# Block two's recurrence input and gate tiles: joint passes over the high part of the weights

## The chip, the cores and the metric

One Trainium2 chip, of which the kernel uses one core. The metric is the device time of one execution in microseconds. Below, PE (TensorE) multiplies matrices, PEld is its weight load, ACT is ScalarE, DVE is VectorE, POOL is GpSimd, and SP issues the DMA loads.

## What is computed

Two blocks, each run for two layers, on 256 tokens of width 1024. The change touches only the mixer of block two, of which this matters (f32 throughout):

```python
def rms_norm_2(x, g):
    xf = x.astype(jnp.float32)
    y = xf * lax.rsqrt(jnp.mean(xf * xf, axis=-1, keepdims=True) + EPS)
    return (y * g.astype(jnp.float32)).astype(x.dtype)
...
        h = rms_norm_2(x, mix_norm[i])
        proj = h @ w_in[i]
        rx, rgate, q, k, v, f_logit, ga, gb = jnp.split(proj, split_idx, axis=-1)

        rx = causal_dwconv(rx, conv_w[i], conv_b[i])
        ya = rg_lru(rx, rg_wa[i], rg_ba[i], rg_wx[i], rg_bx[i], rg_lambda[i])
        ya = (ya * jax.nn.gelu(rgate)) @ w_rnn_out[i]
        yb = forgetting_attention(q, k, v, f_logit, f_b[i], q_norm[i], k_norm[i]) @ w_attn_out[i]
```

`rx` is the input of the recurrence and `rgate` its gate: 1024 columns each of the product with `w_in`. `rg_lru` begins with two block-diagonal products of `rx` and a sigmoid on each. The feed-forward layers stand before and behind the mixer, and the first block has a mixer of its own; neither is touched.

## The kernel before

**Weights.** All weights come in tiles of 128 x 2048 numbers (1 MB). A tile goes through a fixed line: SP loads it into one of four `raw` buffers (L448) once the tile four places earlier has been used; ACT copies it to `hi`, rounded to the type fp32r (`pump`, L1125); DVE subtracts to get the rest, `lo`, into the place of `raw` (`pump`, L1671); then PE may use it. The activations are held the same way, x = x_hi + x_lo. A product is hi·x_hi + hi·x_lo + lo·x_hi. `pump(n)` on ACT or DVE makes all tiles up to number n, at that place of the engine's instruction stream; every engine works strictly through its own stream, and waits on semaphores.

**Form B.** A tile that gives 256 output features by 256 tokens is multiplied in one of two ways. `form_b` (L556) keeps both halves of 128 features in one PSUM bank; for each half and each of eight slices of the contraction it runs three matmuls of 256 columns (L578 to L580), 48 in all. `joint_b` (L583) gives each half of the features its own bank, two banks in all. x_hi and x_lo lie side by side, so one matmul of 512 columns (L592) multiplies the high weights with both, eight for each half; then eight of 256 columns (L595) add lo·x_hi on the left half of the bank, 32 in all. The left half then holds hi·x_hi + lo·x_hi and the right half hi·x_lo, and someone must add them: ACT copies the right halves out (`low_half`), DVE adds them to the left ones (`both_halves`). `joint_b` is used before in the feed-forward layers and for most tiles of the output mixer.

**The stretch.** In block two, each layer runs: feed-forward in and out, `va` (2 tiles), `rx` (4 tiles, recurrence input), `rg` (4 tiles, gate), `fl` (a narrow one, 8 columns), then eight block-diagonal pairs of matmuls (L1048, the products of `rg_lru`), then `q`, `k`, `vb`. In this text rx0 to rx3 and rg0 to rg3 are the tiles of the two jobs, q0 to q3 those of `q`.

- PE: rx0 to rx3 in banks 0 to 3, rg0 to rg3 in banks 0 to 3 again, `fl` in bank 0, all by `form_b`. L1048 for feature group f goes to bank 4 + f % 4, once the convolution of f is there and, from f = 4 on, once ACT has read the bank (`rg_ev`). q0 and q1 write banks 2 and 3.
- DVE: for tile j, first `used(tile)`: `pump` two tiles ahead, then wait for PE. Then a multiply with the row of 1/rms (`times_root`, L1721). For `rx` the convolution follows (L2200, L2203: eight instructions on 256 columns), for `rg` nothing. After `fl` the forget gate's arithmetic (from L2215).
- ACT: for `rx` only its `pump`; then two small functions for the decay (L1556, L1557); for each `rg` tile `pump` two ahead, wait for DVE's multiply, gelu in place (L1562). Then `pump` to q1, and 16 sigmoids on the L1048 products (L1568), of which the first needs its function table loaded.
- After the sigmoids DVE makes `la` and `ii` (L2221, L2222), ACT takes the tanh of `la` (L1572) and only then pumps q2, which DVE turns to `lo` and PE multiplies.

The order on each engine is the order of the code, written by hand. `take(b)` makes PE wait for what last released bank b.

Of the kernel before, what the change touches and what calls it, by code (L numbers as in the profile page):

```python
# [14 lines left out]
P = 128  # L15
# [45 lines left out]
    "gl_ready": (4, 4), "mg_in": (8, 8), "xf_ready": (0, 0), "sum_in": (33, 53), "half_ev": (33, 53),  # L61
# [129 lines left out]
def build_program(nc, dram):  # L191
# [3 lines left out]
    with ctx:  # L195
# [231 lines left out]
        def halves(b, n):  # L427

            return banks[b // 2][:].rearrange("p (f n s) -> p f n s", f=2, n=2)[:, :, n, :]

# [112 lines left out]
        def _(pe):  # L543
# [477 lines left out]
            for layer in range(DEPTH):  # L1021
# [13 lines left out]
                for name in ("rx", "rg"):  # L1035
                    for b, tile in enumerate(BY2[name]):
                        form_b(tile, x_in, b)
                        freed[b] = scaled.next()
                form_b(BY2["fl"][0], x_in, 0)
                freed[0] = scaled.next()  # L1040
# [75 lines left out]
        def _(act):  # L1116
            made, layer_tiles = [0], [None]

            def pump(upto):

                while made[0] <= min(upto, len(layer_tiles[0]) - 1):
                    tile = layer_tiles[0][made[0]]
                    act.wait_ge(*landed(tile))
                    high, of = parts(tile, hi)
                    act_fn(high, of, ACT.Copy).then_inc(hi_done.up(), 1)  # L1125
                    made[0] += 1
# [414 lines left out]
            for layer in range(DEPTH):  # L1541
# [10 lines left out]
                pump(BY2["rx"][2].index + 2)  # L1552
# [5 lines left out]
                for j, tile in enumerate(BY2["rg"]):  # L1558
                    pump(tile.index + 2)
                    act.wait_ge(*scaled.at(5 + j))  # L1560
                    gate = gl[:, 2 * j:2 * j + 2, :]
                    act_fn(gate, gate, ACT.Gelu_apprx_tanh).then_inc(gl_ready.up(), 1)  # L1562
# [99 lines left out]
        def _(dve):  # L1662
# [11 lines left out]
            def used(tile):  # L1674

                pump(tile.index + 2)
                dve.wait_ge(*tile_used.at(tile.index + 1))
# [498 lines left out]
            for layer in range(DEPTH):  # L2176
# [10 lines left out]
                    ALU.subtract).then_inc(lru_v.up(), 1)  # L2187
                for j, tile in enumerate(BY2["rx"]):
                    used(tile)
                    if j == 0:  # L2190
                        dve.wait_ge(*root_out.next())
                    times_root(rxp[:, 2 * j:2 * j + 2, 3:3 + S], bank[j][:], scaled)
# [17 lines left out]
                for j, tile in enumerate(BY2["rg"]):  # L2210
                    used(tile)
                    times_root(gl[:, 2 * j:2 * j + 2, :], bank[j][:], scaled)

                used(BY2["fl"][0])
                tt(fz[:], bank[0][:, 0:S], root_row[:], ALU.mult).then_inc(scaled.up(), 1)  # L2215
# [189 lines left out]
```

## Time and profile before

| | us |
|---|---|
| median of 3 runs (2341.78 to 2343.35) | 2341.84 |
| the profiled execution | 2342.44 |
| its span on the core | 2340.6 |

PE is busy for 98% of the span, at a mean granted clock of 0.995 of full speed. One instruction of the code makes one matmul record, two for the f32 matmuls of L1048. Matmuls overlap: a matmul of 512 columns shows 0.39 us but the next starts 0.23 us later, so a tile's time is read from the starts, not from the durations. On ACT and DVE the next instruction also starts a little before the shown end (0.08 us or so). The profile gives, for every instruction that waited, how long its engine had been idle and what ended that.

### The profile page before, as it was taken

How to read it: one execution, taken by the hardware profiler on the slowest of the kernel's cores; microseconds unless marked ns; L12 is line 12 of the kernel's file. 1: busy time of each engine (PE TensorE's matmuls, PEld its weight loads, DVE VectorE, ACT ScalarE, POOL GpSimd, SP SyncE). 2: the span in 40 equal slices, each digit the busy share in tenths (PEclk: the TensorE clock that was granted, in tenths of full speed). 3: DMA queues.
4: the chain of work that ended last, by engine and by line, in shares of the span. 5: the costliest groups of instructions: out<-in, count | busy, mean ns of one | idle time of the engine just before them, and what ended most of it. 6: DMA issues, size and time to landing. Idle time of an engine off the chain costs nothing.

```text
span 2340.6 us, 31098 instructions
## 1 busy us (share of the span) xinstructions
PE 2295.8 (98%) x13048; PEld 1997.9 (85%) x13048; DVE 1582.7 (68%) x1799; ACT 1319.7 (56%) x1791; POOL 39.0 (2%) x66
## 2 busy tenths in 40 slices
PE   8999999999999999989999999999999999999998
PEld 8878888878888888878898888888888898988886
DVE  5966766568767766657576766675676578666755
ACT  5665565465654654655446755554554458555554
POOL 1000000010000000010000000000100000000000
PEclk9999999999999999999999999999999999999999
DMA  7515565556325655555554355555665645455553
GB/s 246 189 59 162 188 200 188 181 190 205 126 91 191 202 182 188 193 182 192 194 183 160 127 180 189 181 196 173 200 208 175 211 146 180 129 191 177 188 189 117
DMA packets 323132, 412.58 MB, mean 176 GB/s; under 512 B 9361, under 2 KB 245009, under 8 KB 322993
## 3 DMA queue, kind: packets, MB, share of 16 engines
q1 hardware_dynamic: 318160, 395.47, 51.4%
q0 software_dynamic: 4544, 14.12, 2.0%
q8 instruction: 104, 1.70, 0.3%
q10 hardware_dynamic: 288, 0.99, 0.1%
q14 instruction: 36, 0.29, 0.0%
HBM read 409.51 MB, written 1.05 MB: 175 GB/s over the span
## 4 chain that ended last, share of the span: by engine, by line
PE 79%; DVE 11%; ACT 8%; issue 1%; DMA 1%; SPq 0%; DVEq 0%; ACTq 0%
PE banks L592 23%; PE banks L595 12%; PE banks L655 9%; PE banks L656 9%; PE banks L657 9%; DVE lo L1671 5%; ACT hi L1125 4%; PE banks L578 3%; PE banks L579 3%; PE banks L580 3%; PE banks L706 1%; DMA raw<-in_w_in 1%; ACT prob L1293 1%; DVE mg L1817 1%; PE banks L839 1%
## 5 line engine op out<-in xcount | busy, mean ns | idle before, releaser
L1671 DVE TENSOR_TENSOR lo<-raw,hi 128x2048 fp32r<-128x2048 f32 (+1 forms) x384 | 860.9, 2245 | 571.3 <-ACT hi L1125 571.0
L1125 ACT ACTIVATE hi<-raw 128x2048 fp32r<-128x2048 f32 (+1 forms) x384 | 717.1, 1872 | 215.1 <-DMA raw<-in_ffn_w_out 84.0
L592 PE MATMUL banks<-x_in,hi 128*128 128x512 f32 x2304 | 577.5, 392 | 1.3 <-issue 1.2
L592 PEld LDWEIGHTS banks<-x_in,hi 128*128 128x128 f32 x2304 | 414.3, 189 | 76.2 <-issue 1.5
L595 PEld LDWEIGHTS banks<-x_in,lo 128*128 128x128 f32 x2304 | 314.3, 190 | 22.5
L595 PE MATMUL banks<-x_in,lo 128*128 128x256 f32 x2304 | 321.2, 282 | 0.0
L578 PE MATMUL banks<-x_in,hi 128*128 128x256 f32 x752 | 217.0, 289 | 0.0
L579 PE MATMUL banks<-x_in,hi 128*128 128x256 f32 x752 | 214.5, 285 | 0.0
L580 PE MATMUL banks<-x_in,lo 128*128 128x256 f32 x752 | 214.4, 285 | 0.0
L655 PE MATMUL banks<-hi,x_hid 128*128 128x512 f32 x528 | 206.0, 390 | 0.0
L656 PE MATMUL banks<-lo,x_hid 128*128 128x512 f32 x528 | 205.5, 389 | 0.0
L657 PE MATMUL banks<-hi,x_hid 128*128 128x512 f32 x528 | 205.5, 389 | 0.0
L1219 ACT ACTIVATE half<-banks 128x512 f32<-128x512 f32 x120 | 71.5, 596 | 151.1 <-PE banks L595 151.1
L578 PEld LDWEIGHTS banks<-x_in,hi 128*128 128x128 f32 x752 | 146.1, 194 | 2.0 <-issue 1.9
L579 PEld LDWEIGHTS banks<-x_in,hi 128*128 128x128 f32 x752 | 146.2, 194 | 0.1
L580 PEld LDWEIGHTS banks<-x_in,lo 128*128 128x128 f32 x752 | 146.1, 194 | 0.0
L655 PE MATMUL banks<-hi,x_in 128*128 128x512 f32 x320 | 127.0, 397 | 1.9 <-DVE lo L1671 1.9
L657 PE MATMUL banks<-hi,x_in 128*128 128x512 f32 x320 | 124.7, 390 | 0.0
L656 PE MATMUL banks<-lo,x_in 128*128 128x512 f32 x320 | 124.7, 390 | 0.0
L657 PEld LDWEIGHTS banks<-hi,x_hid 128*128 128x128 f32 x528 | 99.1, 188 | 20.7
L655 PEld LDWEIGHTS banks<-hi,x_hid 128*128 128x128 f32 x528 | 99.1, 188 | 20.3
L656 PEld LDWEIGHTS banks<-lo,x_hid 128*128 128x128 f32 x528 | 99.2, 188 | 20.1
(338 smaller groups left out, 3114.1 us busy)
## 6 DMA issues: line engine op xcount, KB each, us to landing
raw<-in_w_in SPq DMA_DIRECT2D x108, 1024.0 KB, 5.1
raw<-in_ffn_w_in SPq DMA_DIRECT2D x88, 1024.0 KB, 5.1
raw<-in_w_ffn_in SPq DMA_DIRECT2D x44, 1024.0 KB, 5.1
raw<-in_ffn_w_out SPq DMA_DIRECT2D x40, 1024.0 KB, 5.0
raw<-in_w_ffn_out SPq DMA_DIRECT2D x20, 1024.0 KB, 5.1
raw<-in_w_o_gla SPq DMA_DIRECT2D x8, 1024.0 KB, 5.2
raw<-in_w_o_attn SPq DMA_DIRECT2D x8, 1024.0 KB, 5.2
raw<-in_w_out SPq DMA_DIRECT2D x8, 1024.0 KB, 5.1
```

Source lines behind the costliest of these rows:

```text
L578: pe.matmul(to, wh[:, k, cut], x[:, k, 0, :], start=(k == 0), stop=False)
L579: pe.matmul(to, wh[:, k, cut], x[:, k, 1, :], start=False, stop=False)
L580: mm = pe.matmul(to, wl[:, k, cut], x[:, k, 0, :], start=False, stop=(k == tile.kc - 1))
L592: pe.matmul(to, wh[:, k, cut], x[:, k, :, :].rearrange("p n s -> p (n s)"), start=(k == 0), stop=(k == KD - 1), skip_group_check=True)
L595: mm = pe.matmul(to[:, 0:S], wl[:, k, cut], x[:, k, 0, :], start=False, stop=(k == KD - 1), skip_group_check=True)
L655: pe.matmul(to, xh, wh[:, k, :], start=(first and k == 0), stop=False)
L656: pe.matmul(to, xh, wl[:, k, :], start=False, stop=False)
L657: mm = pe.matmul(to, xl, wh[:, k, :], start=False, stop=(last and k == tile.kc - 1))
L706: mm = pe.transpose(bank[b][:, k * P:(k + 1) * P], src[:, t, f * P:(f + 1) * P], ident)
L1125: act_fn(high, of, ACT.Copy).then_inc(hi_done.up(), 1)
L1219: act_fn(half[:, i % 2, :].rearrange("p (f s) -> p f s", f=2), halves(joint_bank(first_bank, i), 1), ACT.Copy).then_inc(half_ev.up(), 1)
L1671: tt(rest, of, parts(tile, hi)[0].bitcast(F32), ALU.subtract).then_inc(lo_done.up(), 1)
```

## The change

For the eight tiles of `rx` and `rg` in each of block two's layers, `form_b` becomes `joint_b`. `rx` now uses the pairs of banks beginning with 0, 6, 4, 0 and `rg` those beginning with 6, 4, 2, 0; a pair is released by DVE's addition. ACT gets a copy of the right halves per tile (`low_half`), before the gelu of the same tile and, for `rx`, between its pumps, which are no longer made in one go. It also waits for the addition two tiles earlier, whose buffer it overwrites. DVE gets an addition per tile ahead of the multiply, and waits for ACT's copy where it waited for PE. `fl` goes to bank 2 instead of 0. Two totals of semaphores are raised.

```diff
@@ tensor engine
-                for name in ("rx", "rg"):
-                    for b, tile in enumerate(BY2[name]):
-                        form_b(tile, x_in, b)
-                        freed[b] = scaled.next()
-                form_b(BY2["fl"][0], x_in, 0)
-                freed[0] = scaled.next()
+                for name, first in (("rx", rx_bank), ("rg", rg_bank)):
+                    for b, tile in zip(first, BY2[name]):
+                        joint_b(tile, x_in, b)
+                        freed[b] = freed[b + 1] = sum_in.next()
+                form_b(BY2["fl"][0], x_in, 2)
+                freed[2] = scaled.next(9)
@@ scalar engine
-                pump(BY2["rx"][2].index + 2)
+                sums = 2 * (FF // 256) - 2
+
+                def low_half(i, tile, b):
+                    pump(tile.index + 2)
+                    act.wait_ge(*tile_used.at(tile.index + 1))
+                    if i >= 2:
+                        act.wait_ge(*sum_in.at(sums + i - 1))
+                    act_fn(mix_half[2][:, i % 2, :].rearrange("p (f s) -> p f s", f=2), halves(b, 1),
+                           ACT.Copy).then_inc(half_ev.up(), 1)
+
+                for j, tile in enumerate(BY2["rx"]):
+                    low_half(j, tile, rx_bank[j])
                 act.wait_ge(*par_in.at(8))
 ...
                 for j, tile in enumerate(BY2["rg"]):
-                    pump(tile.index + 2)
+                    low_half(4 + j, tile, rg_bank[j])
                     act.wait_ge(*scaled.at(5 + j))
@@ vector engine
+                def both_halves(to, i, tile, b):
+                    pump(tile.index + 2)
+                    dve.wait_ge(*half_ev.next())
+                    tt(to, halves(b, 0), mix_half[2][:, i % 2, :].rearrange("p (f s) -> p f s", f=2),
+                       ALU.add).then_inc(sum_in.up(), 1)
+                    dve.wait_ge(*sum_in.now())
+                    tt(to, to, root_row[:].unsqueeze(1).broadcast_to([P, 2, S]), ALU.mult).then_inc(scaled.up(), 1)
+
                 for j, tile in enumerate(BY2["rx"]):
-                    used(tile)
                     if j == 0:
                         dve.wait_ge(*root_out.next())
-                    times_root(rxp[:, 2 * j:2 * j + 2, 3:3 + S], bank[j][:], scaled)
+                    both_halves(rxp[:, 2 * j:2 * j + 2, 3:3 + S], j, tile, rx_bank[j])
 ...
                 for j, tile in enumerate(BY2["rg"]):
-                    used(tile)
-                    times_root(gl[:, 2 * j:2 * j + 2, :], bank[j][:], scaled)
+                    both_halves(gl[:, 2 * j:2 * j + 2, :], 4 + j, tile, rg_bank[j])
 
                 used(BY2["fl"][0])
-                tt(fz[:], bank[0][:, 0:S], root_row[:], ALU.mult).then_inc(scaled.up(), 1)
+                tt(fz[:], bank[2][:, 0:S], root_row[:], ALU.mult).then_inc(scaled.up(), 1)
```

On ACT, from the gate tiles to the first sigmoid in block two's first layer; `hi_61` is the high part of rg3, `hi_58` of `fl`, `hi_59` of q0, `hi_60` (the last one) of q1. Before:

```order
L1562 ACT_TABLE_LOAD
L1562 ACTIVATE gl<-gl 128x512 [waits scaled]
L1125 ACTIVATE hi_61<-raw_57 128x2048 [waits raw_in3]
L1562 ACTIVATE gl<-gl 128x512 [waits scaled]
L1125 ACTIVATE hi_58<-raw_54 128x1024 [waits raw_in0]
L1562 ACTIVATE gl<-gl 128x512 [waits scaled]
L1125 ACTIVATE hi_59<-raw_55 128x2048 [waits raw_in1]
L1562 ACTIVATE gl<-gl 128x512 [waits scaled]
L1125 ACTIVATE hi_60<-raw_56 128x2048 [waits raw_in2]
L1568 ACT_TABLE_LOAD [waits rg_full]
L1568 ACTIVATE rr<-banks,pk_122 128x256 [waits tile_used]
```

Now, the same place from the second gate tile on (`mix_half_115` is the copy of the right halves):

```order
L1576 ACTIVATE gl<-gl 128x512 [waits scaled]
L1128 ACTIVATE hi_61<-raw_57 128x2048 [waits raw_in3]
L1562 ACTIVATE mix_half_115<-banks 128x512 [waits sum_in,tile_used]
L1576 ACTIVATE gl<-gl 128x512 [waits scaled]
L1128 ACTIVATE hi_58<-raw_54 128x1024 [waits raw_in0]
L1562 ACTIVATE mix_half_115<-banks 128x512 [waits sum_in,tile_used]
L1576 ACTIVATE gl<-gl 128x512 [waits scaled]
L1128 ACTIVATE hi_59<-raw_55 128x2048 [waits raw_in1]
L1562 ACTIVATE mix_half_115<-banks 128x512 [waits sum_in,tile_used]
L1576 ACTIVATE gl<-gl 128x512 [waits scaled]
L1128 ACTIVATE hi_60<-raw_56 128x2048 [waits raw_in2]
L1582 ACT_TABLE_LOAD [waits rg_full]
```

A copy now stands between each `hi` and the gelu that follows it; the `hi` of the tile two ahead still stands behind the gelu of the tile before.

On DVE, the first recurrence tile (`lo_65` belongs to rx3). Before:

```order
L1671 TENSOR_TENSOR lo_64<-raw_56,hi_60 128x2048 [waits hi_done]
L1721 TENSOR_TENSOR rxp<-banks,root_row 128x2x256 [waits root_out,tile_used]
L2200 TENSOR_SCALAR y<-rxp,pk_122 128x256 [waits scaled]
L2200 TENSOR_SCALAR y<-rxp,pk_122 128x256
L2203 SCALAR_TENSOR_TENSOR y<-rxp,pk_122,y 128x256 [waits dve_step]
L2203 SCALAR_TENSOR_TENSOR y<-rxp,pk_122,y 128x256
```

Now:

```order
L1685 TENSOR_TENSOR lo_64<-raw_56,hi_60 128x2048 [waits hi_done]
L2205 TENSOR_TENSOR rxp<-banks,mix_half_115 128x2x256 [waits half_ev]
L2208 TENSOR_TENSOR rxp<-rxp,root_row 128x2x256 [waits sum_in]
L2221 TENSOR_SCALAR y<-rxp,pk_122 128x256 [waits scaled]
L2221 TENSOR_SCALAR y<-rxp,pk_122 128x256
L2224 SCALAR_TENSOR_TENSOR y<-rxp,pk_122,y 128x256 [waits dve_step]
```

The multiply, which waited for PE (`tile_used`), is behind an addition that waits for ACT (`half_ev`), and all that DVE does afterwards stands one instruction later for each tile. The `lo` of later tiles are among it.

## Rows read from the trace of the kernel before

**Rows 1.** The page: busy time by engine; the chain that ended last, by engine.
```profile
PE 2295.8 (98%) x13048; PEld 1997.9 (85%) x13048; DVE 1582.7 (68%) x1799; ACT 1319.7 (56%) x1791; POOL 39.0 (2%) x66
...
PE 79%; DVE 11%; ACT 8%; issue 1%; DMA 1%; SPq 0%; DVEq 0%; ACTq 0%
```

**Rows 2.** Timeline of PE (start us, duration, engine, line): joint tile, then rx0, rx1.
```profile
1060.69 2.00 PE L592 MATMUL banks<-x_in,hi 128*128 128x512 f32 x8
...
1066.28 2.00 PE L592 MATMUL banks<-x_in,hi 128*128 128x512 f32 x8
...
1203.66 0.36 PE L578 MATMUL banks<-x_in,hi 128*128 128x256 f32 x1
...
1209.50 0.28 PE L578 MATMUL banks<-x_in,hi 128*128 128x256 f32 x1
```

**Rows 3.** Line and tile views: the copy, the addition and the multiply of joint tiles.
```profile
L1219 ACT ACTIVATE half<-banks x120: 574/598/603, 314.5 to 2240.2; 128x512 f32<-128x512 f32 x120
...
L1738 DVE TENSOR_TENSOR sg<-banks,half x60: 682/691/692, 316.2 to 2235.3; 128x512 f32<-128x512 f32 x60
L1721 DVE TENSOR_TENSOR sg<-sg,root_row x60: 691/693/694, 316.9 to 2236.0; 128x512 f32<-128x512 f32 x60
```

**Rows 4.** Timeline of DVE: rx0; rg0 and rg1; rg3; the forget gate.
```profile
1209.70 0.69 DVE L1721 TENSOR_TENSOR rxp<-banks,root_row 128x512 f32<-128x512 f32 x1 [0.53 <-PE banks L580]
...
1213.83 2.29 DVE L1671 TENSOR_TENSOR lo<-raw,hi 128x2048 fp32r<-128x2048 f32 x1
...
1235.42 0.68 DVE L1721 TENSOR_TENSOR gl<-banks,root_row 128x512 f32<-128x512 f32 x1
1238.61 2.29 DVE L1671 TENSOR_TENSOR lo<-raw,hi 128x2048 fp32r<-128x2048 f32 x1 [2.50 <-ACT hi L1125]
1240.82 0.68 DVE L1721 TENSOR_TENSOR gl<-banks,root_row 128x512 f32<-128x512 f32 x1
...
1250.02 0.69 DVE L1721 TENSOR_TENSOR gl<-banks,root_row 128x512 f32<-128x512 f32 x1 [0.25 <-PE banks L580]
...
1255.43 0.42 DVE L2215 TENSOR_TENSOR fz<-banks,root_row 128x256 f32<-128x256 f32 x1
```

**Rows 5.** Timeline of ACT: gelu of rg0; q1's high part; first sigmoids.
```profile
1236.14 0.63 ACT L1562 ACTIVATE gl<-gl 128x512 f32<-128x512 f32 x1 [6.67 <-DVE gl L1721]
...
1251.29 1.90 ACT L1125 ACTIVATE hi<-raw 128x2048 fp32r<-128x2048 f32 x1
1253.81 1.28 ACT L1568 ACT_TABLE_LOAD   x1 [0.62 <-PE banks L1048]
...
1255.48 0.47 ACT L1568 ACTIVATE ii<-banks,pk 128x256 f32<-128x256 f32 x1
```

**Rows 6.** Timelines of PE and DVE behind the gates: L1048, q0, q2.
```profile
1252.70 7.08 PE L1048 MATMUL banks<-y,bd 128*128 128x256 f32 x32
1259.43 0.58 PE L655 MATMUL banks<-hi,x_in 128*128 128x512 f32 x1
...
1271.01 0.50 PE L655 MATMUL banks<-hi,x_in 128*128 128x512 f32 x1 [0.32 <-DVE lo L1671]
...
1268.66 2.29 DVE L1671 TENSOR_TENSOR lo<-raw,hi 128x2048 fp32r<-128x2048 f32 x1 [3.09 <-ACT hi L1125]
```

**Rows 7.** The same places in block two's second layer.
```profile
1914.65 0.69 DVE L1721 TENSOR_TENSOR gl<-banks,root_row 128x512 f32<-128x512 f32 x1
...
1918.44 1.28 ACT L1568 ACT_TABLE_LOAD   x1 [0.62 <-PE banks L1048]
```

**Rows 8.** PE's longest wait (timeline), and windows around it: busy, PEclk, DMA.
```profile
1001.82 1.11 PE L706 MATMUL banks<-cst,xn 128*128 128x128 f32 x4 [6.26 <-DVE xn L1710]
...
999.00:1002.00 3.00, 0.18 (x1) 0.18 (x2) 2.93 (x6) 1.62 (x6) 0.00 (x0) 0.66 0.01 3
1002.00:1005.00 3.00, 2.22 (x10) 1.85 (x11) 1.81 (x3) 1.90 (x5) 0.00 (x0) 0.50 0.00 0
1005.00:1008.00 3.00, 3.00 (x20) 3.00 (x20) 0.13 (x1) 1.26 (x5) 0.00 (x0) 0.70 0.02 5
```

More of the change, by code:

```diff
@@ L60 @@
     "root_ready": (2, 4), "root_full": (2, 3), "root_out": (2, 3), "gate_in": (11, 22), "scaled": (9, 9),
-    "gl_ready": (4, 4), "mg_in": (8, 8), "xf_ready": (0, 0), "sum_in": (33, 53), "half_ev": (33, 53),
+    "gl_ready": (4, 4), "mg_in": (8, 8), "xf_ready": (0, 0), "sum_in": (33, 61), "half_ev": (33, 61),
 }
@@ L429, in halves @@
             return banks[b // 2][:].rearrange("p (f n s) -> p f n s", f=2, n=2)[:, :, n, :]
+        rx_bank, rg_bank = (0, 6, 4, 0), (6, 4, 2, 0)
         def mixer_bank(j, i):
```

## The prediction, made before the changed kernel was timed

> **What bounds the kernel now.** I read the page first, for the share of each engine and the chain that ended last. PE is busy for 98% of the span and makes 79% of the chain [rows 1]: time is saved only where PE's own work becomes shorter, and lost wherever PE must wait longer. Next comes the timeline of the stretch that the change touches, engine by engine. PE runs through the eight tiles of `rx` and `rg` without a gap, one every 5.76 us (48 matmuls, 0.12 us apart; rx0 starts at 1203.66, rx1 at 1209.50, 0.08 us of this being the start behind another kind of matmul [rows 2]). What matters is how close DVE and ACT are behind it. In `rx` DVE's turn for one tile is the multiply and the convolution, 1209.70 to 1213.83, or 4.13 us, and a `lo`, after which the next instruction starts 2.21 us later (1238.61 to 1240.82) [rows 4]. That is 6.34 us against PE's 5.76: DVE already loses ground in `rx` and lives on its start. In `rg` there is a ring: gelu of a tile on ACT, `hi` of a later tile, `lo` of it on DVE, the multiply of the next gate tile, and its gelu. At 1250.02 and at 1253.81 the ring is just about even with PE: DVE has waited 0.25 us for rg3, and ACT 0.62 us for the first L1048 product [rows 4, 5]. These two waits are all the slack there is at the end of the ring.
>
> Behind it PE depends on ACT. Sigmoids of group 0 end at 1255.95 (1255.48 + 0.47), and feature group 4 of L1048 needs that bank [rows 5]. L1048 takes 6.73 us for eight groups, 0.84 each (1252.70 to 1259.43), so group 4 comes at 1256.06, 0.1 us after it may, and then q0 starts [rows 6]. The last sigmoid leads to `la`, the tanh, the `hi` of q2 and its `lo` at 1268.66, for which PE waits 0.32 us at 1271.01 [rows 6]. So a delay of the first sigmoid above 0.1 us delays q0, and one of any size delays q2.
>
> **TensorE's part.** A joint tile takes 5.59 us (1060.69 to 1066.28, in which two halves of eight matmuls of 512 and eight of 256 columns begin [rows 2]). The columns are the same, 16 x 512 + 16 x 256 = 48 x 256, and 16 starts fewer save 0.17 us, 16 tiles 2.7 us. This is the whole gain that the change can have, if nothing waits: 0.12% of the time.
>
> The Trainium skill ("TensorE: Matmul & The Clock Gate", section Back-to-back issue gap) gives a warm matmul N/2.4 + about 2.5 ns; by it 16 starts fewer would be worth 0.04 us a tile and 0.6 us in all, an estimate from that page. The trace disagrees: 120 ns for 256 columns and, from the tile, (5.59 - 16 x 0.12)/16 = 229 ns for 512 columns, so a start costs about 11 ns, and 0.17 us a tile stands.
>
> **DVE's part.** Each tile gets an addition, 0.69 us, and the multiply behind it starts about 0.72 us after the addition's start, as it must see its result (durations 0.691 and 0.693 [rows 3], and 0.03 us for the wait). The multiply now reads the sum instead of PSUM: 0.693 against 0.68, nothing. So all that DVE does after tile j is 0.72 x (j + 1) later: 5.76 us after the eight tiles.
>
> **ACT's part.** A copy per tile, 0.60 us [rows 3]. Only the first is in DVE's way: rx0 is used 0.17 us sooner, the copy and its hand-over take 0.65, so DVE starts its turn at 1210.2 instead of 1209.70 [rows 4], +0.5 us. Later copies are made while DVE works on the `lo` before (2.21 us), behind a tile that PE has finished long ago. The decay's two functions move behind rx3's copy; PE is through with rx3 at 1203.74 + 4 x 5.59 + 0.2 = 1226.3, the copy ends at 1226.9, and DVE asks for them only at 1236, after four of its turns. The copy buffer is free each time, since its addition came a whole tile earlier. SP's loads stand as before: a buffer is given back when PE has used it, at most 2 us earlier or later.
>
> **The schedule carried forward, first layer.** The multiply of rg0 was at 1235.42 [rows 4]; its addition is now at 1235.42 + 0.5 + 4 x 0.72 = 1238.8. The `lo` of rg2 stands right before it and ends at 1238.9, but PE wants rg2 at 1203.74 + 6 x 5.59 = 1237.3: here PE waits 1.7 us. The gelu of rg0 is at 1236.14 + 0.5 + 5 x 0.72 = 1240.2 [rows 5], and every member of the ring follows from the one before: gelu and `hi` 2.47 (1236.14 to 1238.61), `lo` 2.21 (to 1240.82), addition 0.72, multiply and hand-over 0.72 (1235.42 to 1236.14) [rows 4, 5], together 6.12 us a round, where it was 5.40 and PE's tile is 5.59 us. So the ring is now slower than PE. The `lo` of rg3 ends at 1240.2 + 2.47 + 2.29 = 1245.0; PE, having begun rg2 at 1239.0, would like it at 1244.6: 0.5 us more. At the end of the ring the delay is 0.5 + 8 x 0.72 = 6.26 us, less the two waits that it swallows, 0.25 (DVE for rg3 [rows 4]) and 0.62 (ACT for L1048 [rows 5]): the sigmoids' table load starts at 1253.81 + 5.4 = 1259.2. PE meanwhile is through with rg3 at 1245.1 + 5.6 = 1250.7, with `fl` (24 matmuls, 2.88 us) at 1253.6 and with groups 0 to 3 of L1048 at 1256.9, and stands until ACT has read group 0, 1255.95 + 5.4 = 1261.35. q0 starts 4 x 0.84 later, at 1264.7, against 1259.43 [rows 6]: +5.3. The chain by `la` and q2 is 5.4 later. PE has no gap afterwards in which this could be made good (0.32 us at q2, which the same chain causes), so 5.3 to 5.4 us go to the end. Since it is the ring that decides, the 0.17 us a tile on PE bring nothing.
>
> **Second layer.** The same rows with the same waits (0.62 us before the table load at 1918.44) [rows 7]; DVE's multiply of rx0 there stood right behind a `lo`, so the copy costs 0.4 instead of 0.5, and the rest is alike: 5.3 us.
>
> **Bank 2 for `fl`.** q0 writes banks 2 and 3 and must now wait for DVE's multiply on bank 2, L2215, which stands behind the `lo` of q1. That multiply was at 1255.43 [rows 4] and goes with it to 1259.2 + 2.21 = 1261.4, and ends at 1261.8; q0 could start at 1264.7 at the earliest. Nothing as long as the ring stays late by 5 us; without the sigmoids' delay this wait would itself be the next thing, 1261.8 against 1259.4.
>
> **Sum.** 2 x 5.35 = 10.7 us. The profiled execution took 2342.4 (span 2340.6), which gives 2353.1; the median of the three runs is 0.6 lower and gives 2352.5. I say 2353. The terms have bounds: hand-over 0 to 0.1 us a tile (additions 0.68 to 0.80 apart), the swallowed waits 0 to 1 us in a layer; so 2350.5 to 2355 for this case alone.
>
> **Rivals.**
> (1) *The clock.* The forecast leaves PE idle for 4.4 us (1256.9 to 1261.35) in each layer. In the trace, an idle time of 6.26 us is followed by a granted clock of 0.66, 0.50 and 0.70 in three windows of 3 us [rows 8]: some 6.8 us at 1.2 instead of 2.4 GHz, of which PE's work loses at most half, 3.4 us. Between that wait and waits of about 1 us the trace has none inside the kernel's work, so 4.4 us may do it or not. Against it speaks that the idle time is a third shorter. If it comes in both layers, it costs 1.0 to 3.4 us each: 2354.5 to 2359.5, centre 2356.
> The same page of the Trainium skill (section Why this matters for your kernels) warns that idle gaps between bursts of matmuls bring the halved clock back. By it this rival would be the forecast, 2356; the trace agrees for 6.26 us and is silent on 4.4.
> (2) *Other side: not slower.* PE alone decides and the ring has more room than I count: if DVE and ACT kept ahead of PE, the gain of 2.7 us would show, 2339.1. It decides at rg2: its `lo` would have to be ready by 1237.3. For it speaks that PE waits nowhere in this stretch before; against it that the margin, counted in rows, is 0.87 us at the end of the ring and 6.26 are put in.
> (3) *Half hidden.* If some of the additions fell into time in which DVE waits for `hi` (2.50 us before the `lo` at 1238.61 [rows 4]), only the five up to rg0 would count, 0.5 + 5 x 0.72 - 0.87 = 3.2 us a layer: 2348.3. I think not, since that `hi` waits for the gelu, and the gelu for the multiply behind the addition.
>
> **How the numbers follow.** Forecast 0.60, the clock 0.22, half hidden 0.06, not slower 0.08, and 0.04 for a delay beyond these. What a measurement can tell from no change is 0.2%, 4.7 us: slower means above 2346.5, faster below 2337.2. Slower holds the forecast, the clock, nearly all of half hidden and the rest beyond: 0.91. Not slower at 2339.1 is within 0.2% of before: 0.08 with what is left of half hidden. Faster 0.01. For 8 in 10 the range takes the forecast's own, most of the clock's and some of half hidden: 2348.5 to 2358.
>
> **What would show it.** In the profile of the changed kernel: joint tiles 5.59 us apart on PE in `rx`; PE waiting for `lo` at rg2 (about 1.7 us) and rg3 (0.5); gelus 6.1 us apart; the sigmoids' table load without any wait for PE, 5.4 us later than before against rx0's start; PE waiting 4.4 us for ACT inside L1048; and no wait of q0 for DVE. The prediction is wrong if PE's wait inside L1048 is under 2 us, if an addition costs DVE clearly other than 0.72 us, or if the granted clock falls after the wait.

## The result, and the profile after

| us | before | after |
|---|---|---|
| median of four runs | 2341.8 (2340.9 to 2343.4) | 2365.9 (2362.3 to 2368.3) |
| profiled execution | 2342.4 | 2365.0 |
| its span | 2340.6 | 2363.2 |

The ratio is 1.0102, with a 95% interval of 1.0086 to 1.0118: the changed kernel is 24 us slower (20 to 28). The direction was forecast. The size was not: 10.7 us were forecast, and 2365.9 lies above the whole range of 2348.5 to 2358.0.

The page of the changed kernel, busy time and then the chain, beside [rows 1]:

```profile
PE 2298.3 (97%) x12792; PEld 1986.2 (84%) x12792; DVE 1593.4 (67%) x1815; ACT 1328.7 (56%) x1807; POOL 38.8 (2%) x66
...
PE 75%; DVE 14%; ACT 8%; issue 2%; DMA 1%; SPq 0%; DVEq 0%; ACTq 0%
```

TensorE has 256 matmuls fewer and yet is busy 2.5 us longer, a first sign that some of them ran slower. PE's share of the chain is down from 79% to 75% and DVE's up from 11% to 14%: TensorE waits for DVE now. The view of waits, grouped by line (sum in us, count, longest), has two rows for PE that the kernel before has nothing like:

```profile
PE banks L595 <- DVE lo L1685: 10.6, 6, 3.5
...
PE banks L1051 <- ACT ii L1582: 8.3, 2, 4.2
```

The second is the wait that was forecast (L1051 is L1048 of before). The first has six waits and not four, and the longest is 3.5 us. Here is PE in the timeline (start, duration), from the root row over rx0, rg2 and rg3 to q0, with the second layer's last wait at the end; [rows 2, 6] are the same places of before:

```profile
1200.68 0.61 PE L735 MATMUL banks<-cst,small 128*128 128x128 f32 x4
1204.80 3.13 PE L595 MATMUL banks<-x_in,hi 128*128 128x512 f32 x8 [3.51 <-DVE lo L1685]
...
1241.62 2.11 PE L595 MATMUL banks<-x_in,hi 128*128 128x512 f32 x8 [1.50 <-DVE lo L1685]
...
1247.74 2.11 PE L595 MATMUL banks<-x_in,hi 128*128 128x512 f32 x8 [0.27 <-DVE lo L1685]
...
1256.31 3.61 PE L1051 MATMUL banks<-y,bd 128*128 128x256 f32 x16
1264.09 5.15 PE L1051 MATMUL banks<-y,bd 128*128 128x256 f32 x16 [4.16 <-ACT ii L1582]
1268.88 0.58 PE L658 MATMUL banks<-hi,x_in 128*128 128x512 f32 x1
...
1940.46 6.57 PE L1051 MATMUL banks<-y,bd 128*128 128x256 f32 x16 [4.16 <-ACT ii L1582]
1946.68 0.59 PE L658 MATMUL banks<-hi,x_in 128*128 128x512 f32 x1
```

The waits at rg2 and rg3 and the one inside L1048 are those of the forecast. Two things are not. PE stands for 3.51 us before rx0, and no such wait was in the sum. And work behind the two long waits is slow: rx0's first eight matmuls take 3.13 us, where the joint tiles of [rows 2] take 2.00, and the second half of L1048 takes 5.15 and 6.57 us, where the first half takes 3.61. Windows show why (length, then busy time of PE, PEld, DVE, ACT and POOL, then the granted clock, DMA share, GB/s); the first is rx0's first half, the second L1048's second half with the start of q0:

```profile
1204.80:1209.25 4.45, 4.45 (x16) 3.83 (x17) 4.35 (x2) 0.00 (x0) 0.00 (x0) 0.62 0.13 42
...
1264.09:1269.20 5.11, 5.11 (x17) 4.32 (x18) 1.43 (x5) 4.51 (x12) 0.00 (x0) 0.71 0.02 5
```

The granted clock is 0.62 and 0.71 there, a mixture of 2.4 and 1.2 GHz. PE is busy all the time and does less.

The wait before rx0 is explained by DVE's and ACT's timelines at that place:

```profile
1202.04 0.38 ACT L1215 ACTIVATE root_row<-banks 128x256 f32<-128x256 f32 x1
```

```profile
1202.45 6.70 DVE L1685 TENSOR_TENSOR lo<-raw,hi 128x2048 fp32r<-128x2048 f32 x3 [7.66 <-ACT root_row L1215]
```

DVE has stood for 7.66 us and then makes the low parts of rx0, rx1 and rx2 one after the other. What it waits for is ACT's copy of the root row, which a `lo` does not read. In the kernel before, DVE had made two of the three `lo` ahead of this place, those of rx0 and rx1, before ACT copied the root row at 1204.66:

```profile
1197.75 2.29 DVE L1671 TENSOR_TENSOR lo<-raw,hi 128x2048 fp32r<-128x2048 f32 x1 [0.32 <-ACT hi L1125]
1200.42 2.29 DVE L1671 TENSOR_TENSOR lo<-raw,hi 128x2048 fp32r<-128x2048 f32 x1 [0.38 <-ACT hi L1125]
```

The order of DVE's instructions shows the cause. Before:

```
L1671 TENSOR_TENSOR lo_62<-raw_54,hi_58 128x2048 [waits hi_done]
L1671 TENSOR_TENSOR lo_63<-raw_55,hi_59 128x2048 [waits hi_done]
L1671 TENSOR_TENSOR lo_64<-raw_56,hi_60 128x2048 [waits hi_done]
L1721 TENSOR_TENSOR rxp<-banks,root_row 128x2x256 [waits root_out,tile_used]
```

Now:

```
L1685 TENSOR_TENSOR lo_62<-raw_54,hi_58 128x2048 [waits hi_done,root_out]
L1685 TENSOR_TENSOR lo_63<-raw_55,hi_59 128x2048 [waits hi_done]
L1685 TENSOR_TENSOR lo_64<-raw_56,hi_60 128x2048 [waits hi_done]
L2205 TENSOR_TENSOR rxp<-banks,mix_half_115 128x2x256 [waits half_ev]
```

`used(tile)` makes the high and low parts that are due (`pump`) and then waits for the tile. It stood ahead of the wait for `root_out`. The change takes `used(tile)` away and puts its `pump` into `both_halves`, which stands behind that wait. The line with the wait is not a changed line of the diff; what stands on its two sides is.

One table follows all the kernels below through this stretch. Times are us from the start of the root row's matmuls (1203.30 before, 1200.68 after in the first layer), so that a different start of the stretch doesn't count. Where the layers differ by over 0.05 us both are given. The last column is the difference of the medians to the kernel before on the same chip, with the 95% interval of the ratio turned into us.

| kernel | rx0 | L1048 begins | sigmoids' table load | PE's wait in L1048 | q0 | q0 later, both layers | measured |
|---|---|---|---|---|---|---|---|
| before | 0.36 | 49.40 | 50.51 | none | 56.13 | | |
| after | 4.12 | 55.63 | 61.13 | 4.16 | 68.20 / 69.65 | +25.6 | +24.1 (20.1 to 27.6) |
| e1_lo_first | 0.36 | 50.42 | 55.93 | 4.18 | 64.41 / 64.34 | +16.5 | +14.8 (12.2 to 18.7) |
| e2_wait_only | 4.12 | 54.66 | 55.76 | none | 61.39 | +10.5 | +12.1 (9.4 to 15.2) |
| e3_dve_only | 0.36 | 50.01 | 55.35 | 4.01 | 62.40 / 62.68 | +12.8 | +12.2 (10.5 to 16.4) |
| e4_gelu_late | 0.36 | 49.89 | 50.99 | none | 56.61 | +1.0 | +0.2 (-1.6 to 2.6) |
| e5_filled | 0.36 | 50.43 | 55.92 | 0.57 | 61.48 | +10.7 | +11.1 (8.4 to 14.5) |
| e6_conv_late | 0.36 | 48.02 | 49.13 | none | 54.75 | -2.8 | -3.7 (-5.6 to -1.4) |
| e7_joint_only | 0.36 | 48.02 | 49.39 | none | 55.01 | -2.3 | -2.2 (-4.5 to -0.2) |
| e8_order_only | 0.36 | 49.40 | 50.51 | none | 56.13 | 0.0 | +0.5 (-1.9 to 2.3) |
| e9_wait_filled | 4.12 | 53.18 | 54.28 | none | 59.90 | +7.5 | +7.5 (4.5 to 9.4) |
| e10_late_only | 4.12 | 55.15 / 54.87 | 56.26 / 55.98 | none | 61.88 / 61.60 | +11.2 | +11.6 (7.3 to 13.6) |

Reading the start of q0 in two places of one profile gives each measured difference within its interval, so the stretch from the root row to q0 holds all of the effect that can be told from noise.

### The profile page after: what moved, and what is told of

Its sections match the earlier page's. It is cut to its first block, busy times and chain, and to the rows that moved or that the text cites. A ratio compares the mean times of both kernels' runs of the same rounds, so it can differ in the third digit from the quotient of the medians.

```text
span 2363.2 us, 30632 instructions
## 1 busy us (share of the span) xinstructions
PE 2298.3 (97%) x12792; PEld 1986.2 (84%) x12792; DVE 1593.4 (67%) x1815; ACT 1328.7 (56%) x1807; POOL 38.8 (2%) x66
## 4 chain that ended last, share of the span: by engine, by line
PE 75%; DVE 14%; ACT 8%; issue 2%; DMA 1%; SPq 0%; DVEq 0%; ACTq 0%
PE banks L595 23%; PE banks L598 12%; PE banks L658 9%; PE banks L659 9%; PE banks L660 9%; DVE lo L1685 6%; ACT hi L1128 4%; PE banks L581 2%; PE banks L582 2%; PE banks L583 2%; DVE y L2224 1%; PE banks L709 1%; DMA raw<-in_w_in 1%; DVE mg L1831 1%; ACT prob L1296 1%
## 5 line engine op out<-in xcount | busy, mean ns | idle before, releaser
L595 PE MATMUL banks<-x_in,hi 128*128 128x512 f32 x2560 | 644.6, 394 | 11.9 <-DVE lo L1685 10.6
L595 PEld LDWEIGHTS banks<-x_in,hi 128*128 128x128 f32 x2560 | 461.6, 189 | 96.6 <-DVE lo L1685 12.3
L598 PEld LDWEIGHTS banks<-x_in,lo 128*128 128x128 f32 x2560 | 350.3, 191 | 25.2
L598 PE MATMUL banks<-x_in,lo 128*128 128x256 f32 x2560 | 357.7, 283 | 0.0
L581 PE MATMUL banks<-x_in,hi 128*128 128x256 f32 x496 | 142.4, 287 | 0.0
L583 PE MATMUL banks<-x_in,lo 128*128 128x256 f32 x496 | 140.3, 283 | 0.0
L582 PE MATMUL banks<-x_in,hi 128*128 128x256 f32 x496 | 140.3, 283 | 0.0
L659 PEld LDWEIGHTS banks<-lo,x_hid 128*128 128x128 f32 x528 | 99.2, 188 | 20.1
L1233 ACT ACTIVATE sg<-sg 128x512 f32<-128x512 f32 x66 | 41.7, 632 | 118.1 <-DVE sg L1735 118.1
L581 PEld LDWEIGHTS banks<-x_in,hi 128*128 128x128 f32 x496 | 95.1, 192 | 1.6 <-issue 1.4
L582 PEld LDWEIGHTS banks<-x_in,hi 128*128 128x128 f32 x496 | 95.1, 192 | 0.1
```

Source lines behind the costliest of these rows:

```text
L581: pe.matmul(to, wh[:, k, cut], x[:, k, 0, :], start=(k == 0), stop=False)
L582: pe.matmul(to, wh[:, k, cut], x[:, k, 1, :], start=False, stop=False)
L583: mm = pe.matmul(to, wl[:, k, cut], x[:, k, 0, :], start=False, stop=(k == tile.kc - 1))
L595: pe.matmul(to, wh[:, k, cut], x[:, k, :, :].rearrange("p n s -> p (n s)"), start=(k == 0), stop=(k == KD - 1), skip_group_check=True)
L598: mm = pe.matmul(to[:, 0:S], wl[:, k, cut], x[:, k, 0, :], start=False, stop=(k == KD - 1), skip_group_check=True)
L659: pe.matmul(to, xh, wl[:, k, :], start=False, stop=False)
```

## The experiments

**e1_lo_first** puts the `lo` back ahead of the wait and leaves the rest of the change as it is.

```diff
                 for j, tile in enumerate(BY2["rx"]):
                     if j == 0:
+                        pump(tile.index + 2)
                         dve.wait_ge(*root_out.next())
                     both_halves(rxp[:, 2 * j:2 * j + 2, 3:3 + S], j, tile, rx_bank[j])
```

> The changed kernel, with DVE's wait for the row of 1/rms (root_out) put behind its pump again, so that the lo of rx0 to rx2 no longer wait for it. Theory A (the changed kernel loses in each layer 3.8 us to that wait, 1.65 us to the halved clock behind it, 5.2 us to the ring of ACT and DVE with its additions, and 1.4 to 2.9 us to a halved clock inside the L1048 products): 2 x 5.4 = 10.8 us less than the changed kernel, about 2355; PE starts rx0 0.36 us behind the root row's matmuls, at full clock; the wait of about 4.2 us inside L1048 stays. Theory B (the ring and the clock explain all; the lo were early enough anyway): 2366 as before.

Measured: 2358.2, ratio 1.0066 (1.0052 to 1.0080). rx0 starts 0.36 us behind the root row again, and 9.3 of the 24.1 us are gone. What is left is more than the 10.7 us of the forecast. PE's timeline, second half of L1048 and q0, then a window of that half:

```profile
1262.48 6.56 PE L1051 MATMUL banks<-y,bd 128*128 128x256 f32 x16 [4.18 <-ACT ii L1582]
...
1268.68 0.58 PE L658 MATMUL banks<-hi,x_in 128*128 128x512 f32 x1
```

```profile
1262.48:1268.70 6.22, 6.22 (x17) 5.00 (x17) 1.43 (x5) 4.45 (x12) 0.00 (x0) 0.53 0.01 4
```

The wait of 4.18 us is the forecast's 4.4. Behind it the granted clock is 0.53 for the whole half, which takes 6.20 us to q0 where four groups at full clock take 3.36: 2.8 us that the forecast didn't have. In the first layer of the changed kernel the same half lost 1.4 us. That difference is why this edit gave back 9.1 us by the two places of q0 and not the 10.8 that were expected. The clock was at its lower level before the wait was over:

```profile
1262.00:1262.48 0.48, 0.00 (x1) 0.04 (x1) 0.48 (x2) 0.48 (x2) 0.00 (x0) 0.50 0.00 0
```

**e2_wait_only** does the opposite: the kernel before, with the wait moved ahead of the `lo` and nothing else.

```diff
                 for j, tile in enumerate(BY2["rx"]):
-                    used(tile)
                     if j == 0:
                         dve.wait_ge(*root_out.next())
+                    used(tile)
```

> The kernel before, with nothing changed but DVE's wait for root_out, which is put ahead of the pump of rx0's turn. No joint tiles, no additions. Theory A: PE waits 3.5 us for the lo of rx0 and runs the next 3.4 us at half clock, so 3.8 + 1.65 us in each layer, 10.8 in all: 2352.6, with no long wait inside L1048 and no halved clock there. Theory B: at most 1 us, 2342 to 2343.

Measured: 2355.4, ratio 1.0052 (1.0040 to 1.0065). Two lines exchanged cost 12.1 us. PE's timeline at rx0, in the old form with three matmuls of 256 columns in turn:

```profile
1205.44 0.61 PE L732 MATMUL banks<-cst,small 128*128 128x128 f32 x4
1209.56 0.38 PE L578 MATMUL banks<-x_in,hi 128*128 128x256 f32 x1 [3.51 <-DVE lo L1671]
...
1210.61 0.28 PE L580 MATMUL banks<-x_in,lo 128*128 128x256 f32 x1
1210.73 0.38 PE L578 MATMUL banks<-x_in,hi 128*128 128x256 f32 x1
1210.90 0.42 PE L579 MATMUL banks<-x_in,hi 128*128 128x256 f32 x1
1211.12 0.42 PE L580 MATMUL banks<-x_in,lo 128*128 128x256 f32 x1
```

The wait is the same 3.51 us as in the changed kernel, so it has nothing to do with joint tiles. The rows below it show the other part. Up to 1210.73 the matmuls start 0.12 us apart; from 1210.90 on it is 0.21 to 0.22 us. In this layer the clock falls 1.2 us after PE has taken up work again; in the second layer the starts are 0.21 us apart from 1879.88 on, 0.4 us after PE began at 1879.50. At L1048 the delay is 5.26 us: 3.76 from the wait, 1.5 from the clock.

**e3_dve_only** asks whether the ring alone gives the forecast's loss: the kernel before, with one more DVE operation of the addition's size ahead of each of the eight multiplies (it multiplies the same tile into a buffer that nobody reads, and the real multiply waits for it).

The edit for `rx`; that for `rg` is the same:

```diff
+                    times_root(mix_half[2][:, j % 2, :].rearrange("p (f s) -> p f s", f=2), bank[j][:], dve_step)
+                    dve.wait_ge(*dve_step.now())
                     times_root(rxp[:, 2 * j:2 * j + 2, 3:3 + S], bank[j][:], scaled)
```

> The kernel before with form_b throughout, and DVE's multiply made twice for each of the eight tiles (once into a spare buffer, as long as the addition of the change, the second waiting for the first). This is the additions' cost alone: no copies, no joint tiles, the pump where it was. Theory A (ring): 8 x 0.72 - 0.87 = 4.9 us a layer, 9.8 in all, and 0 to 3 us a layer where the wait inside L1048, some 4 us, brings the clock down: 2351.6 to 2357. Rival (DVE is busy for two thirds only, and hides them): 2342.

Measured: 2355.5, ratio 1.0057 (1.0045 to 1.0070). The sigmoids' table load is 4.84 us later. No matmul is changed here and no copy is added, and PE stands in L1048 all the same:

```profile
1260.08 5.12 PE L1048 MATMUL banks<-y,bd 128*128 128x256 f32 x16 [4.01 <-ACT ii L1568]
```

So eight operations of 0.7 us on an engine that is busy for 68% of the span cost about 12 us: 4.84 us in each layer by the later table load, and the rest of q0's 6.3 to 6.6 us by the clock. The gelu of rg0 is already 3.62 us late (36.46 us after the root row against 32.84): five of the eight additions are in the delay before the ring of the gates begins.

**e4_gelu_late** opens the ring. It is e1 with the gelu of each gate tile one tile later on ACT, so that the next tile's `hi` no longer stands behind a gelu that waits for DVE. `gelu(j)` holds the three lines that are taken out.

```diff
                 for j, tile in enumerate(BY2["rg"]):
                     low_half(4 + j, tile, rg_bank[j])
-                    act.wait_ge(*scaled.at(5 + j))
-                    gate = gl[:, 2 * j:2 * j + 2, :]
-                    act_fn(gate, gate, ACT.Gelu_apprx_tanh).then_inc(gl_ready.up(), 1)
+                    if j:
+                        gelu(j - 1)
+                pump(BY2["fl"][0].index + 2)
+                gelu(3)
```

> As e1_lo_first, and ACT makes the gelu of a gate tile one tile later, behind the high part and the copy of the next tile; the last gelu comes behind the high part of q1. DVE and PE have the same work in the same order. Theory A (the round gelu, hi, lo, addition, multiply sets the pace): the round is open, PE waits only for the lo of rg2, 1.7 us, of which 1.3 are gained by shorter tiles; the first sigmoid is 0.3 us later than before the change, no wait inside L1048: about 2342.5. Rival (it is DVE's load in the stretch, whatever ACT's order): little better than e1_lo_first, 2353.

Measured: 2343.5, ratio 1.0002 (0.9993 to 1.0011): of e1's 14.8 us nothing is left that can be told from no change. All additions and copies are still there. The first row below is PE at rg2, the second the whole of L1048, the third ACT's table load:

```profile
1240.24 2.12 PE L595 MATMUL banks<-x_in,hi 128*128 128x512 f32 x8 [1.59 <-DVE lo L1691]
...
1254.41 7.08 PE L1051 MATMUL banks<-y,bd 128*128 128x256 f32 x32
```

```profile
1255.51 1.28 ACT L1588 ACT_TABLE_LOAD   x1 [0.35 <-PE banks L1051]
```

PE no longer waits in L1048, and ACT waits for PE there. DVE comes to rg0 as late as in e1 (its addition starts 35.6 us after the root row in both), but it reaches rg1 3.53 us later and not 6.12, since it no longer stands for 2.50 us before the next `lo`. One wait is left, 1.59 us for the `lo` of rg2: DVE is behind when it comes out of `rx`, with four convolutions and four additions. No fall of the clock follows it.

**e5_filled** takes the clock out of e1 and leaves the wait: while PE would stand in L1048 it does 32 transposes into a free bank, which nobody reads.

```diff
                     pe.wait_ge(*conv_ready.next())
+                    if f == 4:
+                        take(3)
+                        for _ in range(32):
+                            pe.transpose(bank[3][:, 0:P], ident, ident)
                     take(b)
```

> e1_lo_first with 32 transposes of the identity into the free bank 3 on PE between feature groups 3 and 4 of the L1048 products, some 3.7 us of work of no use in the wait of 4.2 us; the result is untouched. Theory A (the wait also brings the clock down, and this costs 2.9 us a layer in the profile of e1_lo_first): groups 4 to 7 take 3.4 us instead of 6.2 to 6.4, granted clock 1.00 there, so up to 5.8 us less than e1_lo_first, 2352 to 2354. Rival (the clock's fall is covered by the wait and costs nothing, or comes all the same): 2358.

Measured: 2353.9, ratio 1.0049 (1.0036 to 1.0062). PE's timeline and a window of the second half:

```profile
1258.80 3.66 PE L1052 MATMUL banks<-cst 128*128 128x128 f32 x32
1263.03 3.72 PE L1055 MATMUL banks<-y,bd 128*128 128x256 f32 x16 [0.57 <-ACT ii L1586]
```

```profile
1263.03:1266.40 3.37, 3.37 (x17) 2.97 (x17) 1.52 (x5) 3.37 (x10) 0.00 (x0) 1.00 0.01 2
```

ACT is as late as in e1 (table load at 55.92 against 55.93), so the dependency is the same. The granted clock is 1.00 and q0 comes at 61.48 and not 64.4: work that is thrown away saves 2.9 us in each layer by the profiles. By the medians it is 3.8 us in all, and the intervals of e1 and e5 overlap (1.0052 to 1.0080 and 1.0036 to 1.0062): the times alone leave the gain open, the starts and the clock show it. And this kernel is the forecast's case, a late ring at full clock: 5.35 us in each layer by the profile, as the sum had it, 11.1 us by the medians.

**e6_conv_late** goes on from e4, at the last wait: the fourth convolution moves on DVE from the end of `rx` to behind rg1's multiply.

```diff
                 for j, tile in enumerate(BY2["rx"]):
...
                     dve.wait_ge(*scaled.now())
-                    for tap in range(3, -1, -1):
...
+                    if j < 3:
+                        conv(j)
...
                     both_halves(gl[:, 2 * j:2 * j + 2, :], 4 + j, tile, rg_bank[j])
+                    if j == 1:
+                        conv(3)
```

> e4_gelu_late, and DVE makes rx3's convolution behind the gate tile rg1 instead of ahead of rg0, so that the lo of rg2 comes 3.4 us sooner. Theory A: PE's last wait in the stretch, 1.6 us for that lo, is gone, and the shorter joint tiles show, 1.36 us a layer: 2.7 us less than the kernel before. Rival (something else is then late, the sigmoids or bank 2): as e4_gelu_late, equal to before.

Measured: 2339.2, ratio 0.9985 (0.9976 to 0.9994): faster than both kernels. PE's timeline has no wait in the stretch:

```profile
1204.11 0.60 PE L735 MATMUL banks<-cst,small 128*128 128x128 f32 x4
...
1252.13 7.08 PE L1051 MATMUL banks<-y,bd 128*128 128x256 f32 x32
1258.86 0.58 PE L658 MATMUL banks<-hi,x_in 128*128 128x512 f32 x1
```

From the root row to L1048 it is 48.02 us, 1.38 less than before: eight joint tiles at 0.17 us. That is the gain the prediction named as the most that the change can have, and it shows as soon as nothing waits.

**e7_joint_only** is joint tiles without their price: PE's part of the change with the kernel before's DVE and ACT. The product of the high part with the input's low part is left out of the result, since nobody adds the second half.

```diff
-                    for b, tile in enumerate(BY2[name]):
-                        form_b(tile, x_in, b)
-                        freed[b] = scaled.next()
+                    for b, tile in zip(rx_bank if name == "rx" else rg_bank, BY2[name]):
+                        joint_b(tile, x_in, b)
+                        freed[b] = freed[b + 1] = scaled.next()
```

> The kernel before with joint_b for rx and rg and nothing else: the right halves of the banks (high weights by the low part of x) are left out of the sums, so there is no copy and no addition, and ACT and DVE work as before. Theory A: PE gains 1.36 us a layer up to fl, but the first sigmoid comes only some 0.9 us sooner, since the ring had 0.87 us of slack, so q0 starts about 0.9 us sooner: 1.7 to 1.8 us less than before. Rival (joint tiles are shorter than 5.59 us here, or longer): read from the tiles.

Measured: 2340.7, ratio 0.9990 (0.9981 to 0.9999). L1048 begins at 48.02, as in e6. But q0 is only 1.12 us earlier than before, because ACT's table load no longer waits for PE and comes at 49.39 where e6 has 49.13; the old chain of DVE and ACT, with nothing added to it, already ends 0.26 us too late for joint tiles.

**e8_order_only** is e6's two moves on the kernel before.

```diff
                 for j, tile in enumerate(BY2["rg"]):
                     pump(tile.index + 2)
+                    if j:
+                        gelu(j - 1)
...
                     times_root(gl[:, 2 * j:2 * j + 2, :], bank[j][:], scaled)
+                    if j == 1:
+                        conv(3)
```

> The kernel before with the two reorderings of e6_conv_late (gelus one tile later on ACT, rx3's convolution behind rg1 on DVE), and form_b as before. A control: both theories expect no change, PE goes through rx and rg without a wait already. If it is faster, the gain of e6_conv_late is not the joint tiles'.

Measured: 2343.3, ratio 1.0001 (0.9992 to 1.0010). PE is where it was to 0.01 us. DVE and ACT have more room than before: ACT waits for PE 2.22 us ahead of the table load in the first layer, 0.96 in the second, where [rows 5] have 0.62:

```profile
1253.74 1.28 ACT L1574 ACT_TABLE_LOAD   x1 [2.22 <-PE banks L1048]
```

So e6's gain is not made by the moves alone; it takes the joint tiles, with the moves as their cover.

**e9_wait_filled** is e2 with 28 transposes on PE between the root row and rx0. It splits e2's loss into the wait and the clock.

```diff
                 roots_to_row(4, root_ready.at(1))
+                take(5)
+                for _ in range(28):
+                    pe.transpose(bank[5][:, 0:P], ident, ident)
```

> e2_wait_only with 28 transposes of the identity into the free bank 5 on PE, behind the root row's matmuls: some 3.2 us of work of no use inside the wait of 3.5 us for the lo of rx0. Theory A: the wait itself stays (3.8 us a layer), the halved clock behind it does not come (1.65 us a layer): 3.3 us less than e2_wait_only, about 7.5 us above before. Rival: the clock's loss there is only beside the wait, same as e2_wait_only.

Measured: 2350.8, ratio 1.0030 (1.0019 to 1.0040). rx0 starts at 4.12 as in e2, and a window of the 4 us behind it has a granted clock of 1.00, where e2 has 0.65 (e9 first, then e2):

```profile
1204.66:1208.66 4.00, 4.00 (x33) 4.00 (x34) 4.00 (x2) 1.92 (x1) 0.00 (x0) 1.00 0.11 37
```

```profile
1209.56:1213.56 4.00, 4.00 (x23) 4.00 (x24) 4.00 (x2) 1.92 (x1) 0.00 (x0) 0.65 0.11 37
```

The wait is worth 3.76 us in each layer and the clock 1.49 (59.90 against 61.39).

**e10_late_only** is the changed kernel with e4's later gelus, and with the `lo` left behind the wait.

```diff
                     low_half(4 + j, tile, rg_bank[j])
+                    if j:
+                        gelu(j - 1)
```

> The changed kernel with the gelus one tile later on ACT, as in e4_gelu_late, and DVE's wait for root_out left where the change puts it, ahead of the pump. Theory A (the two causes add): what is left is the wait for the lo of rx0 and the clock behind it, 5.4 us a layer, as in e2_wait_only; PE's wait for the lo of rg2 stays at 1.6 us, no long wait inside L1048: about 11 to 12 us above before. Rival (the delay at rx0 gives the ring time to catch up, so the two overlap): 5 to 8 us.

Measured: 2354.9, ratio 1.0045 (1.0031 to 1.0058), 11.6 us over before, and e2's 12.1 is the loss of the wait alone. By q0's place it is 11.2 us: 10.5 as in e2, and 1.0 as in e4, less 0.3 us by which the clock cost less at rx0 of the second layer. With the ring open, the first wait remains at its full price: the two losses do not hide each other.

## Why the prediction was wrong

**Where the 24 us are.** By q0's place in the table, the first layer loses 12.07 us and the second 13.52. e2 has 5.26 of that in each layer (the moved wait, 3.76, and the clock behind it, 1.5), e5 has 5.35 (the ring at full clock). The half clock inside L1048 is 1.43 and 2.86: the second half began at 63.41 and 63.43 and q0 comes 4.79 and 6.22 us later, where it should be 3.36. The sums are 12.04 and 13.47. Together 25.5 us; the medians have 24.1, within their interval.

**The step that failed** is the one under "DVE's part", and with it the start of the schedule. It says that each tile gets an addition and that "all that DVE does after tile j is 0.72 x (j + 1) later". It counted what `both_halves` adds and not what the helper had taken in: `pump`, which went behind the wait for `root_out`. The schedule therefore began with rx0 in its old place, and the 2 x 3.76 us, with the 2 x 1.5 us of the clock behind them, were not in the sum, nor in any rival. The other part of the miss is the clock in L1048, 1.4 + 2.9 us, which the sum put at nothing. Together they are 14.8 us, and q0's place shows 25.6 - 10.7 = 14.9. The moved wait could have been read: in the rows of DVE's order that stand ahead of the prediction, `root_out` is in the brackets of the old multiply and in none of the new rows. A wait that leaves one instruction has gone to another, and the new one was not looked up.

**The clock** was the first rival, at 0.22, with 1.0 to 3.4 us in each layer for the wait in L1048. The mechanism and the size were right (1.4 to 2.9), the chance was not: five profiles have twelve waits of 3.5 to 4.2 us in the stretch, and with each of them the clock fell. e1 is this rival's case, 14.8 us above before, where its centre was some 14. The forecast weighed only that 4.4 us is a third less than the 6.26 of [rows 8]. It also read all three windows of [rows 8] as behind that wait. The first lies almost wholly in it, and the clock had fallen while PE still stood:

```profile
1000.00:1001.82 1.82, 0.00 (x0) 0.00 (x0) 1.75 (x5) 0.74 (x3) 0.00 (x0) 0.50 0.00 0
```

The Trainium skill ("TensorE: Matmul & The Clock Gate", section Why this matters for your kernels) warns that idle gaps between bursts of matmuls bring the halved clock back. By it both waits would be expected to cost clock, and the traces agree at 3.51 us and above; at 1.6 us they show no fall.

**Of the rest, nearly all held.**
- Joint tiles: eight of them save 1.38 us by e6 (8 x 0.17). The other price, 0.04 us a tile, an estimate from the Trainium skill ("TensorE: Matmul & The Clock Gate", section Back-to-back issue gap), would have given 0.3; the trace had rightly been preferred.
- Ring: gelus 6.12 us apart were forecast, for every round. ACT's timeline of the changed kernel has the gelus of rg0 to rg3:

```profile
1242.92 0.63 ACT L1576 ACTIVATE gl<-gl 128x512 f32<-128x512 f32 x1 [6.45 <-DVE gl L2208]
...
1249.04 0.63 ACT L1576 ACTIVATE gl<-gl 128x512 f32<-128x512 f32 x1 [3.20 <-DVE gl L2208]
...
1253.24 0.63 ACT L1576 ACTIVATE gl<-gl 128x512 f32<-128x512 f32 x1 [2.13 <-DVE gl L2208]
...
1259.36 0.63 ACT L1576 ACTIVATE gl<-gl 128x512 f32<-128x512 f32 x1 [3.20 <-DVE gl L2208]
```

  The rounds are 6.12, 4.20 and 6.12 us; the middle one has the `hi` and `lo` of `fl`, which are half as large. Three rounds take 16.44 us and three joint tiles of PE 16.77, so "the ring is now slower than PE" does not hold over the gates as a whole. The sum came out all the same because it was made of delays: in e1 the gelu of rg0 is 4.19 us late (37.03 against 32.84), by the first copy and five additions, four of them in `rx`, where DVE's turn takes 7.06 us a tile against PE's 5.59. The ring adds the last three and gives back only the two waits of before (0.87 us), as each of its links waits for the one before.

- The addition and the multiply behind it: 0.72 us apart, as summed (DVE's timeline, rg0).

```profile
1241.48 0.68 DVE L2205 TENSOR_TENSOR gl<-banks,mix_half 128x512 f32<-128x512 f32 x1
1242.20 0.69 DVE L2208 TENSOR_TENSOR gl<-gl,root_row 128x512 f32<-128x512 f32 x1
```

- PE's waits: 1.7 and 0.5 us forecast at rg2 and rg3, 1.50 and 0.27 measured; 4.4 in L1048, 4.16 measured.
- Table load 5.4 us later: 5.42 in e1, where rx0 is in its place.
- Bank 2 for `fl`: q0 waits for no DVE operation in any of the kernels.
- The sum, 10.7 us for the ring alone: 10.7 by e5's profile, 11.1 by its medians.
- Half hidden and not slower: e3 and e1 exclude that additions disappear in DVE's idle time while the ring is closed. Once it is open (e4, e6) they do: e6 is 2.8 us faster than before by q0's place and 3.7 (1.4 to 5.6) by the medians, where the rival "not slower" had 2.7.

**What a shown wait leaves out.** In e1 PE needs 2.40 us more than in e6 from rx0 to L1048, and its two waits show only 1.86. The starts of the half tiles hold the rest. Measured from start to start the two waits cost 1.75 and 0.44 us, as the shown idle time begins at the shown end of a matmul, behind the place where the next one could start; and the half tile behind each wait takes 2.90 us and not 2.79. The same is why 3.51 us of idle time put rx0 3.76 us back.

**Left open.** Why the fall lasts through L1048 in the second layer of the changed kernel and through a part of it in the first was not tried.

## What to carry to other kernels

When an edit moves a call into a helper, or a helper past a line that waits, look up for every wait which instruction carries it now, unchanged lines included; two exchanged lines were worth 12 us here, as much as all of the arithmetic that was added. Follow the engines behind TensorE by their delay and not by their busy share. Here DVE fell behind in `rx`, and in the ring of `rg` each link waited for the one before, so that only 0.87 us was made good although three rounds (16.44 us) are shorter than three tiles (16.77 us). Delaying one link by a tile (the gelu) gave back 14.6 of 14.8 us. Then give a forecast wait of TensorE of 3.5 us or more the price of a clock that falls with it, 1.3 to 2.9 us here.

## What the runs showed of the hardware

In the stretch a lower granted clock came with each of the twelve waits of 3.5 to 4.2 us, in five profiles. By windows of about 0.5 us it began between 1.1 us before the wait ended (L1048 in e1, second layer) and 1.3 us behind its end (L1048 in e3, second layer), and it cost 1.3 to 1.6 us at rx0 (behind 3.51 us) and 1.4 to 2.9 us in L1048 (behind 4.0 to 4.2 us). With waits of 1.6 us and less it was never seen in the stretch.

These waits are no threshold. Elsewhere in the profiles eight waits lie between 1.7 and 2.4 us, not counting those at the kernel's start. The clock fell behind two of them (1.80 us at 558.97 in the changed kernel, 2.32 us at 562.24 in e7) and not behind the other six, of 1.75 to 2.09 us. In the kernel before it also fell from 532 to 536, where no wait of PE is shown (two windows of 2 us have 0.59 and 0.56). What decides there was not tested, and such falls differ between two profiles of nearly the same kernel.

Useless transposes in the wait prevented the fall at both places, and were a gain of 2.9 and 1.5 us a layer over standing still by the profiles. By the medians, each taken against the kernel before on its own chip, e5 is 3.8 us faster than e1, a difference that the two intervals leave open, and e9 4.6 us faster than e2. No version with a fill is as fast as one without the wait.
